# Stationary weights for the query and key chunks, and another order at the end of attention, in an eleven-stage transformer kernel on one core

## The reference

```python
qkv = (h @ w_qkv).reshape(B, S, 3, 3, 8, 64)         # three dilation groups, 8 heads of 64
for g, (window, dil) in enumerate(((128, 1), (512, 4), (2048, 16))):
    s = q @ k.T * 64 ** -0.5 + bias                  # T5 buckets, causal, dilated band
    num, den, m = exp(s - max) @ v, sum, max
o = merged num / merged den                          # one softmax over the three groups
h = h + o.reshape(B, S, 512) @ w_out
h = h + square(relu(rms_norm(h) @ w_up)) @ w_down    # the second MLP, "mlp1"
```

## Time and profile before

| | |
|---|---|
| three timed runs | 1518.22, 1518.52, 1518.59 us; median 1518.52 |
| the profiled execution's own time | 1518.72 us |
| its span in the trace | 1517.0 us |
| TensorE busy with matmuls | 1482.4 us (98%) |
| VectorE, ScalarE busy | 1047.3 us (69%), 701.7 us (46%) |
| qkv stage, attention with its output product | 279.8 to 386.1 us, 387.0 to 435.2 us of the span |

### The profile page before, as it was taken

One profiled execution on the slowest core, in us unless ns is written; L12 is line 12 of the kernel. 1 busy time (PEld: TensorE's weight loads), 2 busy tenths in 40 slices (PEclk: granted clock), 3 DMA queues, 4 the chain that ended last, 5 costly groups with the idle time before them and its releaser, 6 DMA issues.

```text
span 1517.0 us, 17499 instructions
## 1 busy us (share of the span) xinstructions
PE 1482.4 (98%) x7110; PEld 1220.5 (80%) x7110; DVE 1047.3 (69%) x1222; ACT 701.7 (46%) x882; POOL 31.0 (2%) x63
## 2 busy tenths in 40 slices
PE   8999999999899999999999999999999999999998
PEld 6778888888678888788888788887888889888886
DVE  6578677776768677778887688787455567665554
ACT  6264454544754444634344533445443453453432
POOL 1000000000000000000000000000000000000000
PEclk9899999999999999999999999999999999999999
DMA  9368878777458878588884488976555555555652
GB/s 326 112 215 302 288 262 285 243 267 257 128 177 294 283 260 323 195 275 307 304 290 127 152 313 305 320 241 208 176 184 186 176 173 181 173 168 192 194 184 80
DMA packets 202284, 346.21 MB, mean 228 GB/s; under 512 B 9643, under 2 KB 105139, under 8 KB 202204
## 3 DMA queue, kind: packets, MB, share of 16 engines
q1 hardware_dynamic: 163836, 269.45, 53.2%
q10 hardware_dynamic: 38368, 75.64, 13.9%
HBM read 343.96 MB, written 1.09 MB: 227 GB/s over the span
## 4 chain that ended last, share of the span: by engine, by line
PE 87%; DVE 6%; ACT 3%; DMA 1%; SPq 1%; issue 1%; POOL 0%; ACTq 0%; DVEq 0%; POOLq 0%
PE up_ps L1499 51%; PE acc L1499 32%; PE tr_ps L1599 3%; DVE w_lo L977 2%; ACT w_hi L568 2%; DVE ada_acc L1073 1%; PE tr_ps L1710 1%; DMA raw<-in_a_w_in 1%; PE tr_ps L1827 1%; ACT xn L613 1%; DVE res L1115 0%; DMA raw<-in_conv_w_in 0%; SPq L398 0%; DVE xn L1112 0%; SPq L417 0%
## 5 line engine op out<-in xcount | busy, mean ns | idle before, releaser
L977 DVE TENSOR_TENSOR w_lo<-raw,w_hi 128x2048 fp32r<-128x2048 f32 x238 | 540.2, 2290 | 196.2 <-ACT w_hi L568 196.2
L568 ACT ACTIVATE w_hi<-raw 128x2048 fp32r<-128x2048 f32 x243 | 457.6, 1915 | 72.7 <-DVE ada_acc L1073 36.9
L1499 PE MATMUL up_ps<-w_hi,xT_hi 128*128 128x512 f32 x1200 | 480.2, 400 | 6.2 <-DVE xT_lo L1026 3.1
L1499 PE MATMUL up_ps<-w_hi,xT_lo 128*128 128x512 f32 x1200 | 470.4, 392 | 0.0
L1499 PE MATMUL up_ps<-w_lo,xT_hi 128*128 128x512 f32 x1200 | 469.6, 391 | 0.0
L1499 PEld LDWEIGHTS up_ps<-w_hi,xT_hi 128*128 128x128 f32 x1200 | 226.7, 189 | 58.6 <-issue 8.1
L1499 PEld LDWEIGHTS up_ps<-w_hi,xT_lo 128*128 128x128 f32 x1200 | 226.3, 189 | 48.8
L1499 PEld LDWEIGHTS up_ps<-w_lo,xT_hi 128*128 128x128 f32 x1200 | 226.9, 189 | 43.8
L1499 PE MATMUL acc<-w_hi,hT_hi 128*128 128x512 f32 x640 | 203.3, 392 | 0.0
L1499 PE MATMUL acc<-w_hi,hT_lo 128*128 128x512 f32 x640 | 202.1, 390 | 0.0
L1499 PE MATMUL acc<-w_lo,hT_hi 128*128 128x512 f32 x640 | 201.9, 390 | 0.0
(11 more groups left out here) (156 smaller groups left out, 961.8 us busy)
## 6 DMA issues: line engine op xcount, KB each, us to landing
raw<-in_ffn_w_in SPq DMA_DIRECT2D x176, 512.0 KB, 4.9
ada_raw<-in_ada_w ACTq DMA_DIRECT2D x72, 1024.0 KB, 7.4
raw<-in_ffn_w_out SPq DMA_DIRECT2D x88, 512.0 KB, 4.7
raw<-in_w_up SPq DMA_DIRECT2D x64, 512.0 KB, 5.6
raw<-in_w_down SPq DMA_DIRECT2D x64, 512.0 KB, 4.4
raw<-in_b_w_qkv SPq DMA_DIRECT2D x36, 512.0 KB, 4.7
raw<-in_conv_w_in SPq DMA_DIRECT2D x24, 512.0 KB, 4.3
raw<-in_a_w_in SPq DMA_DIRECT2D x16, 512.0 KB, 8.6
```

The costliest lines, as they stand in the source:

```text
L568: nc.scalar.activation(w_hi[:, slot, :], raw[:, slot, :], ACT.Copy).then_inc(hi_ready, 1)
L977: nc.vector.tensor_tensor(w_lo[:, slot, :], raw[:, slot, :], w_hi[:, slot, :].bitcast(F32), ALU.subtract).then_inc(lo_ready, 1)
L1499: return nc.tensor.matmul(dst, a, b, start=start, stop=stop, skip_group_check=True)
```

## The change

Queries and keys: only chunk 0 is still done with stationary activations and turned. Chunks 1 to 5 go through `block_chunk`, which moves out of the conv_in stage's code and takes its semaphore as an argument. ScalarE writes them straight from PSUM into `qkT`; for chunks 1 and 2 (queries) it reads each run of 128 tokens backwards (`flipped_pair`). VectorE's copies and TensorE's transposes of these five chunks are gone.

Attention's end: `attend(2)` follows `turn_probs(13)`; token tile 0 of the first output slab runs ahead of `attend(3)`, the first half of token tile 1 behind it, the second half after token tile 0 of slab 1. `out_hi` and `out_lo` of pairs 0 and 1 come an item later, the split of mlp1's first slab moves from item 12 to behind the last `copy_probs`, and on VectorE ahead of `out_lo(3)`.

mlp1: the modulation sums stand in chunks 3 to 6.

```diff
+MOD_FROM = {"mlp1": 3, "ffn0": 2, "ffn1": 2, "ffn2": 2}
 def mid_fill(p, name, c):
-    return p.tr + NORM_FILLS + TT * c + min(max(c - 1, 0), MOD_FILLS * len(MODS.get(name, ())))
+    return p.tr + NORM_FILLS + TT * c + min(max(c + 1 - MOD_FROM.get(name, 0), 0), MOD_FILLS * len(MODS.get(name, ())))
...
-        ("qkv", 18, 9, NORM_FILLS + 6 * TT, 0, 1),
+        ("qkv", 18, 4, NORM_FILLS + TT, 0, 1),
...
+        def flipped_pair(h):
+            whole = up_ps[:, h, :]
+            return bass.AP(tensor=whole.tensor, offset=whole.offset + P - 1, ap=[list(whole.ap[0]), [P, 2 * TT], [-1, P]])
...
 # ScalarE, qkv, for each of the six chunks
-                    nc.scalar.activation(stage[c % 3][:, t, 0:UPN], up_ps[:, t, :], ACT.Copy).then_inc(qkv_copied, 1)
+                for h in range(2):
+                    if h:
+                        act.wait_ge(slab_used, g + 2)
+                    elif c:
+                        act.wait_ge(qk_blocks, c)
+                    else:
+                        act.wait_ge(up0_ready, p.up + 1)
+                    if c == 0:
+                        a = nc.scalar.activation(mid[:, h, :], up_ps[:, h, :], ACT.Copy)
+                    elif c < 3:
+                        dst = qkT[:, 4 * c + 2 * h:4 * c + 2 * h + 2, :].rearrange("p f (t n) -> p (f t) n", n=P)
+                        a = nc.scalar.activation(dst, flipped_pair(h), ACT.Copy)
+                    else:
+                        a = nc.scalar.activation(qkT[:, 4 * c + 2 * h:4 * c + 2 * h + 2, :], pair_of(h), ACT.Copy)
+                    a.then_inc(qkv_copied, 1)
...
 # ScalarE, attention
-                if i >= 8 and i % 4 == 0:
+                if i >= 8 and i % 4 == 1:
                     out_hi(i // 4 - 2)
-                if i == ITEMS - 4:
-                    ahead(at["attn"].slab - 1)
+            out_hi(PAIRS - 2)
             copy_probs(ITEMS - 2)
-            out_hi(PAIRS - 2)
             copy_probs(ITEMS - 1)
+            ahead(at["attn"].slab - 1)
             out_hi(PAIRS - 1)
...
 # VectorE, qkv: the copies into qkT stay for chunk 0 alone
-                for n in ((), (c - 1,), (c - 1, c))[c % 3]:
+                if c == 1:
...
 # VectorE, attention
+                if i >= 8 and i % 4 == 2:
+                    out_lo(i // 4 - 2)
                 normalise(i)
-                if i >= 8 and i % 4 == 1:
-                    out_lo(i // 4 - 2)
+            out_lo(PAIRS - 2)
             ahead(at["attn"].slab - 1)
-            for pair in range(PAIRS - 2, PAIRS):
-                out_lo(pair)
+            out_lo(PAIRS - 1)
...
 # TensorE, qkv
-            for i in range(2):
-                for b in range(3):
-                    c = 3 * i + b
-                    if c == 0:
-                        first_chunk("qkv")
-                    else:
-                        up_chunk(p.slab + 2 * c, free=(qkv_copied, 2 * (c - 1) + 1))
-                    if b:
-                        qk_turn(b - 1, i)
-                qk_turn(2, i)
+            first_chunk("qkv")
+            for c in range(1, 6):
+                block_chunk(p.slab + 2 * c, (qkv_copied, 2 * c - 1, 2 * c), qk_blocks)
+                if c == 1:
+                    for t in range(TT):
+                        turn(mid, t, 0, 4, p.tr + NORM_FILLS + t, flip[:, 0, :])
...
 # TensorE, attention
+            def first_pairs(t, cs=range(2)):
+                pe.wait_ge(lo_ready, at["attn_out"].slab + 1)
+                pe.wait_ge(o_lo, PAIRS // 2)
+                pe.wait_ge(logit_ready, ITEMS)
+                return down_tile(at["attn_out"].slab, t, hT_hi, hT_lo, 0, True, cs)
...
-                if i > 4 and i % 4 == 2:
+                if i % 4 == 2 and 4 < i < ITEMS - 4:
                     attend(i // 4 - 1)
+                if i == ITEMS - 3:
+                    attend(PAIRS - 2)
+            first_pairs(0)
             attend(PAIRS - 1)
-            down_last(p.slab, hT_hi, hT_lo, 0, True, between=lambda: turn_norm("mlp1", 0), pairs=True)
+            first_pairs(1, (0,))
+            g = at["attn_out"].slab + 1
+            pe.wait_ge(lo_ready, g + 1)
+            pe.wait_ge(o_lo, PAIRS)
+            down_halves(g, 0, hT_hi, hT_lo, 2)
+            first_pairs(1, (1,)).then_inc(slab_used, 1)
+            down_halves(g, 1, hT_hi, hT_lo, 2, lambda: turn_norm("mlp1", 0)).then_inc(slab_used, 1)
```

More of the change, by code:

```diff
@@ L143, in mod_of @@
 def mod_of(name, c):
-    m, q = divmod(c - 2, MOD_FILLS)
+    m, q = divmod(c - MOD_FROM[name], MOD_FILLS) if name in MOD_FROM else (-1, 0)
     return (MODS[name][m], q) if 0 <= m < len(MODS.get(name, ())) else (None, None)
@@ L755, in _ @@
             p = at["qkv"]
-            stage = [mid, pre, xn]
             for c in range(6):
@@ L778, in _ @@
                     if t == 0:
-                        act.wait_ge(up0_ready, p.up + 6 + b + 1)
+                        act.wait_ge(up0_ready, p.up + 1 + b + 1)
                     else:
@@ L1534, in up_chunk, with block_chunk @@
                     last.then_inc(slab_used, 1)
+            def block_chunk(g, free, ready):
+                for s in range(2):
+                    slot = (g + s) % RING
+                    pe.wait_ge(lo_ready, g + s + 1)
+                    for n in range(4):
+                        if s == 0 and n % 2 == 0:
+                            pe.wait_ge(free[0], free[1 + n // 2])
+                        for i in range(UPK):
+                            k = s * UPK + i
+                            cols = slice(i * UPN + n * P, i * UPN + (n + 1) * P)
+                            mm(block_of(n), w_hi[:, slot, cols], xT_hi[:, k, :], start=(k == 0 and n % 2 == 0))
+                            mm(block_of(n), w_lo[:, slot, cols], xT_hi[:, k, :])
+                            last = mm(block_of(n), w_hi[:, slot, cols], xT_lo[:, k, :], stop=(k == KT - 1 and n % 2 == 1))
+                        if s == 1 and n == 1:
+                            last.then_inc(ready, 1)
+                    last.then_inc(slab_used, 1)
             def down_tile(g, t, hi, lo, k0, start, cs=range(2), stop=False):
@@ L1566, in down_slab, with down_last @@
                 last.then_inc(slab_used, 1)
-            def down_last(g, hi, lo, k0, start, ready=None, between=None, pairs=False):
+            def down_last(g, hi, lo, k0, start, ready=None, between=None):
                 for t in range(TT):
@@ L1961, in _ @@
             q = at["conv_out"]
[L1963 to L1977, removed]
-                            last.then_inc(block_ready, 1)
-                    last.then_inc(slab_used, 1)
             g = p.slab
             first_chunk("conv_in")
-            block_chunk(g + 2, (conv_copied, 1, 2))
+            block_chunk(g + 2, (conv_copied, 1, 2), block_ready)
             for t in range(TT):
@@ L1995, in _ @@
                 last.then_inc(tr_ready, 1)
-            block_chunk(g + 6, (u_ready, 1, 2))
-            block_chunk(g + 8, (u_ready, 3, 4))
-            block_chunk(g + 10, (conv_gated, 1, 2))
+            block_chunk(g + 6, (u_ready, 1, 2), block_ready)
+            block_chunk(g + 8, (u_ready, 3, 4), block_ready)
+            block_chunk(g + 10, (conv_gated, 1, 2), block_ready)
             g = q.slab
```

15 lines of the change are left out of this document (3 added, 12 removed).

## The result

The changed kernel takes 1508.93 us, the median of five runs, against 1518.52 before: 9.6 us less. Four of the five lie between 1507.88 and 1509.94 us and one, disturbed for no known cause, took 3010.77; without it the median is 1508.4, 10.1 us less, and to that belong the ratio of 0.9934 and its 95% interval, 0.9923 to 0.9946. The forecast was 7.2 us less, 1511.3, with a range of its own of 1509.9 to 1512.6 and one for 8 in 10 of 1509.3 to 1514.0.

A forecast was written before the change was run, and what follows sets the result against it. TensorE was taken as the bound, busy 1482.4 of 1517.0 us. 2.7 (qkv) + 4.5 (attention's end) + 0 (modulation) = 7.2 us off 1518.72 gave 1511.5, median 1511.3; range 1509.9 to 1512.6, 8 in 10 1509.3 to 1514.0.

The forecast's parts named there:

- Part 1: In qkv, chunks 1 to 5 of queries and keys through block_chunk: 2.7 us less.
- the lower end of its bound: In qkv, ScalarE's backward PSUM copy: 0.60 us at the least, 2.4 us at the most; 0.60 taken.
- 6.0 - 3.3 us: In qkv, TensorE's transpose interruptions removed, 6.0 us, less the matmul time added by 256-column steps, 3.3 us.
- Part 2: At attention's end, new order and moved split: 21.3 us against 25.74, 4.5 us less taken, bounds 2.0 and 6.5.
- the two alternating banks: At attention's end, TensorE's transposes wait for bank copies before items 12, 14 and 15: 0.4 + 0.1 + 0.5 us.
- 0.22 for 0.3: At attention's end, attend(2) waits for out_lo(1), which now comes later: forecast 0.3 us.
- 0.8 before the norm: Before turn_norm, TensorE waits for VectorE's chain with only 2.72 us of work in front: 0.8 us.
- rival A: The lower clock stays at attention's end, 1.0 to 1.5 us back: 1512.6 us; chance 0.12.
- Part 3: In mlp1, modulation transposes and sums a chunk later, no TensorE wait before them: zero, bounds +-0.2 us.
- B: ScalarE's chain bounds attention's end, so only the split's 2 us are gained there: 1513.8 us; chance 0.11.
- C: In qkv, block_chunk's weight loads don't hide and the kernel is slower: 1528 us at half-hidden loads; chance 0.03.
- D: Attention's end gains nothing, as attend(2) queued before item 14 costs what the split gave: 1515.8 us; chance 0.04.

The follow-up runs named there:

- second set: Kernel before and changed kernel each run again without any edit: 1518.25 us and 1509.62 us.
- split_moved: Kernel before with only the split of mlp1's first slab moved from item 12 to behind the last copy_probs: 1515.05 us, ratio 0.9982.
- end_alone: Kernel before plus only the diff's changes to attention's end: 1513.52 us, ratio 0.9967.
- rerun_before: Kernel before, run once more without an edit: 1518.25 us, ratio 1.0003.
- before_72_more: Kernel before with 72 of mlp0's 512-column matmuls each split into two of 256: 1518.68 us.
- rerun_after: Changed kernel, run once more without an edit: 1509.62 us, ratio 0.9942.

## Why the prediction was right and where it failed

**Part 1** was right in its terms. Forecast 2.7 us less, measured 2.88. The step of the new form is 0.1202 us (forecast 0.1204), one group of transposes is left, the backward copy costs what a forward one does, the lower end of its bound, and the splits are never waited for. The sum was to be 6.0 - 3.3 us; with 480 x 0.1202 - 54.5 = 3.2 added, 6.1 went.

**Part 2** was right as well: forecast 21.3 us from item 11's transposes to mlp1, measured 21.26. The waits were 0.34 + 0.34 for 1.0 of the two alternating banks, 0.22 for 0.3, and 0.53 for 0.8 before the norm; what they fell short by is in the work between. The clock stayed at 1.00, which speaks against rival A and, for the alternation of transposes and matmuls that stands here, against the rule of the Trainium skill (TensorE: Matmul & The Clock Gate, "Part 4: PE-mode transpose") by which it was to stay low: about half of the work from item 11's transposes to item 15's (405.31 to 411.57) is transposes. The runs add what one trace could not say: the old end lost the clock in every execution traced, for 3.4 or for 6.8 us, and took 47.95 to 49.56 us. The shown one, 48.14, was near its best. Against the median of six old ends, 48.4, and of the new ones, 43.6, the part gives 4.9, not 4.5.

**Part 3** gave 0 to 0.2 us, within its bounds, where nothing is late. But the row that said that nothing waits there was one execution's: in two of seven traces with the old place the transposes waited, for 0.55 and 1.46 us, and in none of seven with the new. In both VectorE had stood over 5 us for a late load, and in none of the seven with the new place for more than 2.2, so that the move takes such a wait away is not shown.

**What failed is the sum.** "2.7 + 4.5 + 0 = 7.2 us" holds the stages that the change rewrites and prices everything behind them at nothing. With the qkv part come 0.27 us at ffn0's entry, in every kernel that has it, and 0.8 to 1.3 in conv_in, in every one without matmuls added in mlp0, and neither is in any of my terms. The range's lower end held "up to 1 us in which a later stretch of low clock may fall otherwise", and that only for chance, not for something that the change does each time. Added up from the stages' medians: 2.9 + 4.9 + 0.15 + 0.3 + 1.0 = 9.2 us, against 9.6 measured in the first set, with an interval of 8.2 to 11.7, and 8.6 in the second. Of the 2 us by which this exceeds the forecast one is the slab in conv_in, 0.3 ffn0's entry, and 0.8 the parts themselves, 0.3 of it because the old end takes 48.4 us in the median and 48.14 in the trace that I read. How far 1508.93 lies below the forecast is in part chance: the second set's 1509.62 is within the wider range and 0.3 us below the narrower.

**The rivals.** B (ScalarE's chain still bounds the end) falls with the waits of 0.34 us; its kernel was in a way `split_moved`, where only the split is gone: 1515.05. That the split alone would be worth its 2.0 us was too low: 3.1, as the full clock comes with it. C falls: at a DMA share of 0.80 the step is 0.1202 us. D falls: `end_alone` takes 4.6 us less for the stage.

**Open.** Why ffn0's entry takes 7.59 us and not 7.85 with the qkv part. VectorE's `res` update (L1308, and L1320 after) waits 1.46 us for GpSimd in before and 1.11 in after, and starts 0.46 and 0.10 us after the end of GpSimd's `rstd`; nothing in the traces names what it waited for. With 72 or 114 of mlp0's matmuls split it stays at 7.86 and 7.83, so it isn't simply the place of TensorE's code. Also open: why the load of modulation weights was late in `rerun_before` and `before_72_more`. No version tried beats the changed kernel by what can be measured.

## What to carry to other kernels

Read a change's price in the stages that it rewrites, from rows. But here 200 more matmuls for TensorE also shifted where its code is fetched later on, and in a stage that waits for a slab's last packet that was worth 0.8 to 1.3 us; it could as well have gone the other way. So leave that much in the range, and don't credit it to the change's idea. A long instruction is best moved off a queue where it stands behind a wait: there it cost about its length (1.80 of 1.90 us), and the idle steps perhaps the clock as well.

## What the hardware showed that I had not expected

- A 16 KB piece of code takes about 1 us (966 ns for the one in before's conv_in), and a slab whose packets it meets is complete only when those held up behind it have come: the last at 12.83 instead of 11.7 us.
- Gains at the end of attention don't add: 3.1 us for the split alone, 4.2 for the order alone, 4.6 for both.
- ScalarE reads PSUM backwards in runs of 128 as fast as forwards: 588 against 589 ns for a 128 x 512 copy.
- Where the idle steps went, the low clock went: from 3.4 or 6.8 us in every old end to none at that place in any new one. The same drop can still come elsewhere, as at 389 us in `rerun_after`, where it cost 1.4 us.
